# Stick-breaking attention by running sums of the weights and differences of the values

## What is computed

```python
z = jnp.einsum('bhqd,bhkd->bhqk', qb, k).astype(jnp.float32) * (SB_HD ** -0.5)
strict = kpos[None, :] < qpos[:, None]
log_beta = jax.nn.log_sigmoid(z)
log_keep = jnp.where(strict, jax.nn.log_sigmoid(-z), 0.0)
later = lax.cumsum(log_keep, axis=3, reverse=True) - log_keep
w = jnp.where(strict, jnp.exp(log_beta + later), 0.0)
return jnp.einsum('bhqk,bhkd->bhqd', w.astype(v.dtype), v)
```

## Time and profile before

| | us |
|---|---|
| median of 3 runs (lowest, highest) | 2568.44 (2567.80, 2568.92) |
| the profiled execution | 2567.53 |
| its span | 2565.7 |
| TensorE busy in the span | 2500.0 |
| VectorE busy | 1653.7 |
| ScalarE busy | 948.4 |
| GpSimd busy | 974.8 |

### The profile page before, as it was taken

How to read it: one execution, slowest core, us unless ns; L and a number is a source line. 1 busy time by engine, 2 the same in 40 slices (tenths; PEclk the granted TensorE clock), 3 DMA queues, 4 the chain that set the end, 5 groups by cost and what they waited for, 6 DMA issues and landing times.

```text
span 2565.7 us, 32132 instructions
## 1 busy us (share of the span) xinstructions
PE 2500.0 (97%) x12772; PEld 1981.6 (77%) x12772; DVE 1653.7 (64%) x1765; ACT 948.4 (37%) x1380; POOL 974.8 (38%) x547
## 2 busy tenths in 40 slices
PE   7999998999999999999999999899999999999998
PEld 6777775677888888888877777567878888888887
DVE  6887359557765666655677862875586566666554
ACT  6354147534333333100234341855253333331003
POOL 2000430345655465433520023221565555545333
PEclk9999999999999999999999999999999999999999
DMA  5111210032222222522220112002322222224221
GB/s 181 34 43 18 50 29 2 1 133 81 91 83 91 75 82 87 201 99 99 99 67 9 51 34 46 9 2 75 107 74 82 91 77 80 90 98 181 99 99 67
DMA packets 208295, 193.24 MB, mean 75 GB/s; under 512 B 31249, under 2 KB 180881, under 8 KB 208146
## 3 DMA queue, kind: packets, MB, share of 16 engines
q1 hardware_dynamic: 208146, 191.17, 22.9%
HBM read 147.11 MB, written 44.04 MB: 75 GB/s over the span
## 4 chain that ended last, share of the span: by engine, by line
PE 90%; DVE 7%; issue 1%; ACT 1%; SPq 0%; DMA 0%; DVEq 0%; ACTq 0%
PE ps L242 42%; PE ps L2044 32%; PE ps L1449 2%; DVE sb_keep L1527 2%; PE ps L684 2%; PE ps L1472 2%; PE ps L1908 2%; PE ps L1461 1%; DVE u_lo L298 1%; PE ps L775 0%; PE ps L770 0%; PE ps L1508 0%; PE ps L1172 0%; DVE rope_tmp L1308 0%; DVE mla_q L1306 0%
## 5 line engine op out<-in xcount | busy, mean ns | idle before, releaser
L2163 DVE TENSOR_TENSOR h<-ps,h 128x1024 f32<-128x1024 f32 x176 | 214.6, 1223 | 195.2 <-PE ps L242 192.8
L2005 POOL TENSOR_TENSOR w_a<-w_raw,w_a 128x512 fp32r<-128x512 f32 x110 | 178.3, 1630 | 350.7 <-ACT w_a L1995 350.7
L242 PE MATMUL ps<-u_hi,w_hi 128*128 128x512 f32 x864 | 283.5, 409 | 5.4 <-DVE u_lo L298 4.2
L242 PE MATMUL ps<-u_lo,w_hi 128*128 128x512 f32 x864 | 267.6, 391 | 0.0
L242 PE MATMUL ps<-u_hi,w_lo 128*128 128x512 f32 x864 | 267.1, 390 | 0.0
L2044 PE MATMUL ps<-u_b,w_a 128*128 128x512 f32 x1056 | 254.4, 390 | 0.0
L2044 PE MATMUL ps<-u_t,w_s 128*128 128x512 f32 x1056 | 246.5, 389 | 0.0
L2044 PEld LDWEIGHTS ps<-u_b,w_a 128*128 128x128 f32 x1056 | 199.0, 188 | 41.6
L2044 PEld LDWEIGHTS ps<-u_t,w_s 128*128 128x128 f32 x1056 | 198.2, 188 | 41.2
L226 POOL TENSOR_TENSOR w_hi<-w_raw,ones 128x1024 fp32r<-128x1024 f32 (+1 forms) x35 | 65.0, 1858 | 408.1 <-issue 196.4
L242 PE MATMUL ps<-hidden_hi,down_lo 128*128 128x512 f32 x640 | 197.1, 389 | 0.0
(11 more groups left out here) (386 smaller groups left out, 4948.6 us busy)
## 6 DMA issues: line engine op xcount, KB each, us to landing
w_raw<-w_gate SPq DMA_DIRECT2D x44, 512.0 KB, 3.7
w_raw<-w_up SPq DMA_DIRECT2D x44, 512.0 KB, 4.8
hidden_spill<-hidden_gate SPq DMA_DIRECT2D x44, 512.0 KB, 2.6
w_raw<-w_down SPq DMA_DIRECT2D x44, 512.0 KB, 4.5
hidden_back<-hidden_spill SPq DMA_DIRECT2D x44, 512.0 KB, 4.0
w_raw<-w_in SPq DMA_DIRECT2D x42, 512.0 KB, 3.8
h_spill<-h SPq DMA_DIRECT2D x32, 512.0 KB, 4.2
h<-h_spill SPq DMA_DIRECT2D x32, 512.0 KB, 8.0
```

What stands on the lines that cost most here:

```text
L242: last = nc.tensor.matmul(ps[:, bank0 + half, :], a, b[:, half * HALF:(half + 1) * HALF], start=(k == order[0] and n == 0), stop=(k == ord ...
L2005: nc.gpsimd.tensor_tensor(lo, src, hi.bitcast(F32), ALU.subtract).then_inc(w_lo, 1)
L2163: nc.vector.tensor_tensor(wide(h[:, m, :]), pair(p), wide(h[:, m, :]), ALU.add)\
```

## The change

For the weights w of a query, let W of key k be the sum of w over k and all later keys. Running from the last key to the first, W(k) = keep(k) * W(k+1) + beta(k). The output, the sum of w(k) v(k), is the sum of W(k) (v(k) - v(k-1)), with v(-1) = 0. So the kernel scans for sums, in place, with the sigmoid as the second stream, and TensorE multiplies the sums with differences of values.

- ScalarE makes only the sigmoid of z, into `BW`, one instruction a round; `z_read` counts by one a round.
- VectorE makes `KEEP` = 1 - `BW` with a `tensor_scalar` per head (new function `keeps`), first for both heads, and then scans for both (`scan`). The multiplication goes.
- In `latents` a new function `value_steps` reads the values into `VRAW` (the memory of `KRS`), copies the first column to `VF`, and writes the differences of neighbouring columns to the rest. The transpose waits for it by the semaphore `v_steps`.
- `KEEP` loses its padding and the GpSimd instructions that set it, and a branch for GpSimd that no job took is gone.

```diff
+                def value_steps(pr):
+                    j = JOB[f"sbv{pr}"]
+                    if pr:
+                        dve.wait_ge(v_steps, 2 * pr)
+                    read(f"sbv{pr}", VRAW[:, :])
+                    dve.wait_ge(bank_free[j % 4], j // 4 + 1)
+                    nc.vector.tensor_copy(VF[pr][:, 0:1], VRAW[:, 0:1]).then_inc(v_steps, 1)
+                    nc.vector.tensor_tensor(VF[pr][:, 1:S], VRAW[:, 1:S], VRAW[:, 0:S - 1],
+                                            ALU.subtract).then_inc(v_steps, 1)
...
-                read("sbv1", VF[1][:, :])
+                value_steps(1)
...
-                        pe.wait_ge(z_read, 2 * (r - 1))
+                        pe.wait_ge(z_read, r - 1)
...
+                def keeps(i, j):
+                    n = sb_keys(i) * P
+                    if j == 0:
+                        dve.wait_ge(z_read, last_round(i) + 1)
+                    if i >= 3:
+                        dve.wait_ge(scan_done[j], i - 2)
+                    nc.vector.tensor_scalar(KEEP[i % 3][:, j, 0:n], BW[i % 3][:, j, 0:n], -1.0, 1.0, ALU.mult, ALU.add)\
+                        .then_inc(keep_ready[j], 1)
+
                 def scan(i, j):
                     n = sb_keys(i) * P
-                    t = KEEP[i % 3][:, j, S - n:S][:, ::-1]
-                    dve.wait_ge(z_read, 2 * last_round(i) + 1)
-                    nc.vector.tensor_tensor_scan(t, t, ones[:, 0:1].broadcast_to([P, n]), 1.0,
-                                                 ALU.mult, ALU.mult).then_inc(scan_done, 1)
...
-                        nc.vector.tensor_tensor(BW[i % 3][:, j, 0:n], BW[i % 3][:, j, 0:n],
-                                                KEEP[i % 3][:, j, S - n + 1:S + 1], ALU.mult)\
-                            .then_inc(w_ready_dve[j], 1)
+                    sums = BW[i % 3][:, j, 0:n][:, ::-1]
+                    dve.wait_ge(keep_ready[j], i + 1)
+                    nc.vector.tensor_tensor_scan(sums, KEEP[i % 3][:, j, 0:n][:, ::-1], sums, 0.0,
+                                                 ALU.mult, ALU.add).then_inc(scan_done[j], 1)
...
                     if 1 <= s <= JOBS:
+                        for j in range(2):
+                            keeps(s - 1, j)
                         for j in range(2):
                             scan(s - 1, j)
...
-                            for to, at, sign in ((KEEP, S - n, -1.0), (BW, 0, 1.0)):
-                                nc.scalar.activation(to[s % 3][:, :, at + a:at + e],
-                                                     ps[:, 2 * (r % 2):2 * (r % 2) + 2, 0:e - a], ACT.Sigmoid,
-                                                     scale=sign * SB_SCALE).then_inc(z_read, 1)
+                            nc.scalar.activation(BW[s % 3][:, :, a:e], ps[:, 2 * (r % 2):2 * (r % 2) + 2, 0:e - a],
+                                                 ACT.Sigmoid, scale=SB_SCALE).then_inc(z_read, 1)
```

More of the change, by code:

```diff
@@ L1078, in build @@
         KRS = at_r("rope_key", 28, [P, S])
+        VRAW = KRS
         KH = [at_u(f"mla_k{pr}", 32 * pr, [P, 2, S]) for pr in range(PAIRS)]
@@ L1176, in latents_pe @@
                         src = VF[int(name[-1])]
-                        pe.wait_ge(bank_free[JOB[("sbv" if name[3] == "s" else "vv") + name[-1]] % 4],
-                                   JOB[("sbv" if name[3] == "s" else "vv") + name[-1]] // 4 + 1)
+                        if name[3] == "s":
+                            pe.wait_ge(v_steps, 2 * int(name[-1]) + 2)
+                        else:
+                            pe.wait_ge(bank_free[JOB["vv" + name[-1]] % 4], JOB["vv" + name[-1]] // 4 + 1)
                         for c in range(TT):
@@ L1280, in latents_dve @@
                                                    LRS[:, :], ALU.mult, ALU.mult).then_inc(lat_t, 1)
-                read("sbv0", VF[0][:, :])
+                value_steps(0)
                 for k in range(2):
@@ L1330, in build @@
         JOBS = PAIRS * TT
-        KEEP = [nc.alloc_sbuf_tensor_at(f"sb_keep{i}", [P, 2, S + 8], F32, offset=R0 + 64 * KB + i * 8 * (S + 8))
-                for i in range(3)]
+        KEEP = [at_r(f"sb_keep{i}", 64 + 8 * i, [P, 2, S]) for i in range(3)]
         BW = [at_u(f"sb_weight{i}", 16 * i + 8, [P, 2, S]) for i in range(3)]
         PTS = [[at_r(f"sb_weight_t{i}{j}", 89 + 8 * i + 4 * j, [P, TT, P]) for j in range(2)] for i in range(2)]
-        PM = [[nc.alloc_sbuf_tensor_at(f"mla_prob0{j}", [P, S], F32, offset=R0 + 64 * KB + 16 * (S + 8) + j * 4 * KB)
-               for j in range(2)],
+        PM = [[at_r(f"mla_prob0{j}", 80 + 4 * j, [P, S]) for j in range(2)],
               [at_r(f"mla_prob1{j}", 32 + 4 * j, [P, S]) for j in range(2)]]
         PTM = [[at_r(f"mla_prob_t0{j}", 40 + 4 * j, [P, TT, P]) for j in range(2)],
-               [nc.alloc_sbuf_tensor_at(f"mla_prob_t1{j}", [P, TT, P], F32,
-                                        offset=R0 + 64 * KB + 8 * (S + 8) + j * 4 * KB) for j in range(2)]]
+               [at_r(f"mla_prob_t1{j}", 72 + 4 * j, [P, TT, P]) for j in range(2)]]
         RINV = at_r("mla_inverse", 105, [P, 2, P])
@@ L1353, in build @@
         z_read = sem("z_read")
-        one_set = sem("one_set")
-        scan_done = sem("scan_done")
-        w_ready = sems("w_ready", 2)
-        w_ready_dve = sems("w_ready_dve", 2)
+        scan_done = sems("scan_done", 2)
+        keep_ready = sems("keep_ready", 2)
         s_done = sem("s_done")
@@ L1366, in build, with sums_ready @@
         pv_read = sem("pv_read")
-        def on_vector(i, j):
-            return True
-        def weight_ready(i, j):
-            by = on_vector(i, j)
-            return (w_ready_dve if by else w_ready)[j], sum(on_vector(n, j) == by for n in range(i + 1))
+        def sums_ready(i, j):
+            return scan_done[j], i + 1
         def sb_keys(i):
@@ L1591, in attention_pool @@
             def attention_pool(pool):
-                for i in range(3):
-                    nc.gpsimd.memset(KEEP[i][:, :, S:S + 8], 1.0).then_inc(one_set, 1)
-                pool.wait_ge(one_set, 3)
-                for i in range(JOBS):
-                    n = sb_keys(i) * P
-                    for j in range(2):
-                        if on_vector(i, j):
-                            continue
-                        pool.wait_ge(z_read, 2 * last_round(i) + 2)
-                        pool.wait_ge(scan_done, 2 * i + j + 1)
-                        nc.gpsimd.tensor_tensor(BW[i % 3][:, j, 0:n], BW[i % 3][:, j, 0:n],
-                                                KEEP[i % 3][:, j, S - n + 1:S + 1], ALU.mult)\
-                            .then_inc(w_ready[j], 1)
                 pool.wait_ge(pv_done, JOBS)
@@ L1641, in probabilities @@
                     if i == 0:
-                        act.wait_ge(*weight_ready(JOBS - 2, j))
+                        act.wait_ge(*sums_ready(JOBS - 2, j))
                     act.wait_ge(nm_ready, 2 * i + j + 1)
@@ L1687, in attention_act @@
                             for j in range(2):
-                                act.wait_ge(*weight_ready(JOBS - 3, j))
+                                act.wait_ge(*sums_ready(JOBS - 3, j))
                         if i >= 2:
```

18 lines of the change are left out of this document (7 added, 11 removed).

## The result

| | before | changed |
|---|---|---|
| median (lowest, highest), us | 2568.12 (2567.61, 2568.92) | 2546.72 (2545.64, 2547.78) |
| executions | 4 | 4 |
| the profiled execution | 2567.53 | 2545.64 |
| its span | 2565.7 | 2543.8 |

The ratio is 0.9917 (95% interval 0.9902 to 0.9933): the change takes 21.4 us off. The direction and the place were right; the gain in the stretch was larger than what the prediction called a cap.

A forecast was written before the change was run, and what follows sets the result against it. VectorE was taken to set the pace from the first stick-breaking score round to the first latent-attention score; 6.7 + 0.5 + 1.2 = 8.4 us per layer, 16.8 off 2567.5, plus 0.9 for the median, gave 2551.5 us (range 2548 to 2558).

The forecast's parts named there:

- a cap: TensorE's idle time between first stick-breaking and first latent-attention score, 10.0 us per layer, as the most any edit there gives.
- Which engine bounds the stretch: First stick-breaking score round to first latent-attention score: VectorE sets the pace, 67.5 us busy of 71.6; afterwards TensorE bounds.
- Complement and scan: VectorE per 1024 elements: tensor_scalar 0.686 us in place of the multiplication's 1.22; scan with two streams 2.28 to 2.292.
- The order: VectorE does two complements, then two scans, so each gives way early: 0.12 us for 32 scans, 3.8 us per layer.
- 6.7 + 0.5 + 1.2: TensorE waits saved per layer, in us: for VectorE's multiplication, for the first sigmoids, for ScalarE's copies; sum 8.4.
- The failed step: TensorE's transposes, scores and products stay at 61.6 us of work in the stretch, so TensorE becomes the bound.
- The ScalarE work removed gives nothing besides: 24 ScalarE instructions per layer removed bring no further gain, since ScalarE already waited 15.0 us for TensorE.
- The value differences: After the value projections, VectorE's copy and subtraction cost 0: the subtraction takes the gap and GpSimd's second half-split waits.
- Late subtraction: Rival, chance 0.15: value steps miss the gap beside GpSimd's split, shifting the rotary chain 1.8 us per layer; 2555 us.
- full-price complement: Rival, chance 0.06: tensor_scalar takes 1.22 us per 1024, leaving about 3.5 us gain per layer; 2561.5 us.
- Leftover waits: Rival, chance 0.04: in long jobs late products hold VectorE's copies, and half the 6.7 us may return; 2558 us.
- Slow scan: Rival, chance 0.03: backward two-stream scan takes 1.04 ns more an element, kernel 2 x 5.9 us slower; 2580 us.

The follow-up runs named there:

- heads in turn: Changed kernel with complement and scan of one head, then of the other, in place of both complements first: 2547.83 us, ratio 0.9926.
- the run with both edits: Kernel before without the multiplication of weights and without the sigmoid of z, no complement added, output not the reference's: 2545.55 us, ratio 0.9916.
- second sigmoid back: Changed kernel with a second ScalarE sigmoid a round, into the tile the complement then overwrites: 2556.64 us, ratio 0.9959.
- complement at full price: Changed kernel with the complement made by a two-stream tensor_tensor subtraction in place of tensor_scalar: 2559.18 us, ratio 0.997.
- one sigmoid: Kernel before without the sigmoid of z, the multiplication kept and fed from the scan's tile, output not the reference's: 2566.45 us, ratio 0.9998.
- without the multiplication: Kernel before without VectorE's multiplication of weights, the scan writing the weight tile, both sigmoids kept, output not the reference's: 2558.06 us, ratio 0.9966.

## Why the prediction was right, and where it was wrong

- **Which engine bounds the stretch.** Right. VectorE set the pace; relieved of 12 us it waits for TensorE.
- **Complement and scan.** Right: 0.694 for 0.686 and 2.293 for 2.28 us. VectorE's first instruction to the end of its last is 371.90 to 430.12, 58.2 us with 3.0 of waiting for TensorE in it, so 55.2 of work (13 of the 16 result copies among it) against the 55.6 forecast.
- **The order.** Right on VectorE: forecast 3.8 us, 3.6 with the heads in turn. The sum had no term of its own for it; on TensorE it is worth 1.4 us per layer.
- **The waits.** Forecast 6.7 + 0.5 + 1.2. The 6.7 went whole but for the 0.145 that the list leaves out, the wait for the first sigmoids went from 1.8 to 1.3, and the one for copies from 1.3 to 0.8: 6.7 + 0.5 + 0.5 = 7.7, which is what the idle time fell by (10.02 - 2.30). The 1.2 was 0.7 too high.
- **The failed step** is "Its transposes, scores and products do not change: 61.6 us of work in the stretch", and with it "the cap on what any edit of this stretch can give". The instructions did not change, but their recorded busy time fell by 2.66 us per layer. In its place the runs show that TensorE's recorded busy time holds what each stop costs beyond its idle time. The last column is that cost, taken start to start over the 550 multiplications against the run with both edits, which has 3 waits and 58.72 us busy. It accounts for the busy time of every row within 0.02 us (the clock is 1.00 in all of these). The waits alone do not, since the list leaves out the short ones:

| kernel, first stretch | waits of TensorE | busy us | cost beyond idle, us |
|---|---|---|---|
| changed | 3 | 58.95 | 0.22 |
| heads in turn | 6 | 59.50 | 0.79 |
| second sigmoid back | 7 | 60.44 | 1.73 |
| complement at full price | 11 | 61.19 | 2.48 |
| one sigmoid, and before | 15 | 61.61 | 2.90 |

The sum should have read 7.7 + 2.7 = 10.4 us per layer, 20.7 in both, and 2567.5 - 20.7 + 0.9 = 2547.7, a microsecond above the median. Outside the stretches the profiled execution lost 0.65 us and gained the 1.8 of the set-up, which about makes up that microsecond and is no merit of the change. The step failed without it: the stretches alone gave 20.7 where 16.8 was forecast. The low end of 2548 rested on the same false cap.

- **ScalarE.** "The ScalarE work removed gives nothing besides", argued from its 15.0 us of waiting, was the wrong reading even though it did not enter the sum. That waiting does not keep a second sigmoid from standing in front of a copy that TensorE needs soon: 3.3 of the 3.8 us of such waits come where ScalarE has idle time, the rest between 380 and 400 us, where it would have been full. The prediction had seen this in the 1.3 us of waits for copies, but took it as the whole price. Without the single sigmoid the change would have given about half (2567.27 - 2556.64 = 10.6 us, with the second sigmoid put back). The 6.7 us of waits for VectorE was not VectorE's alone to give.
- **The value differences** cost nothing, by the mechanism forecast, with 0.20 us to spare. Leaving them out and delaying them show both sides.
- **The rivals.** Late subtraction and full-price complement did not happen; where an experiment makes them happen, they cost what was worked out, or nearly. Leftover waits: one of 0.145 us for VectorE was left. Slow scan: no.

## What to carry to other kernels

When two engines are relieved at once, test each alone: the list of waits names only the engine that ends last. The second one behind it, here ScalarE's copies behind a second sigmoid, hardly shows in the kernel before, and neither its share of busy time nor its idle time says what it costs: ask what stands in front of the instruction that is waited for. A pipelined engine's recorded busy time holds the tails that its waits expose, so window length minus busy is not a cap on the gain; compare start-to-start times at a place with a wait and at one without, and multiply by the number of stops, those too short for the list among them. Moving a small instruction by 0.2 us can decide which of VectorE and GpSimd holds up the other, so a free edit beside a GpSimd instruction should be tried late as well.

## What was not expected of the hardware

- A wait of TensorE costs more than its idle row shows: 0.17 us of the mask's tail and 0.05 in the transposes behind it at the place shown, 2.90 us beside the run with both edits over the fifteen stops of the kernel before.
- Where VectorE's and GpSimd's instructions both take two operands from SBUF, they exclude each other for nearly the whole instruction: whoever is first runs to its end, and the other's row grows (1.22 to 2.73 us on VectorE, 1.84 to 2.73 on GpSimd). VectorE's instructions with one operand in PSUM are not held: `rope_key<-ps,rs` takes 1.23 us from 347.66 beside GpSimd's 347.64 to 349.11, and `mla_q<-ps,rope` 1.22 from 350.31 beside its 349.19 to 351.92. And a copy of one column took 0.15 us while GpSimd's split was under way (348.92, under 347.64 to 349.11), where the set-up's copy of four columns had taken 1.82. The Trainium skill, GPSIMD Engine Reference, section Key points, speaks of contention for the shared interfaces; these rows agree for the long subtraction and for the reads from PSUM, and not for the small copy.
- The granted clock fell below 1.00 in some stretches of otherwise like kernels: 0.97 in both layers without the multiplication, 0.97 in one layer of two with the second sigmoid back. With one sigmoid alone the second layer shows 0.98 and 62.61 us busy, yet the stretch is as long as the first (71.38 and 71.39): there the slower clock went into TensorE's waits for VectorE. Each time it is one stretch of 3.4 us at 0.50, the lower level, behind TensorE's wait for the first sigmoids. What sets it off is open, since the kernel before has that wait without it.
